# One ones-product per norm: squares of two RMS norms summed off TensorE in a fused two-block kernel

## The reference, cut to what matters

```
x = x + m @ w_o                                          # first block; the kernel calls this X1
gate = sigmoid(rmsnorm(x, ple_norm_g) @ w_ple_gate)      # the norm "r_ple", over 2048 features
x = x + gate * (p @ w_ple_proj)
...
o = (o_f + o_b)                                          # second block: retention, 4 heads of 256 values
o = o * rsqrt(mean(o * o, axis=-1) + 1e-6)               # the norm "rn", one per head, over its 256 values
```

## Time and profile before

| | before |
|---|---|
| median of 3 runs | 2671.77 us (2671.35 to 2673.11) |
| profiled execution | 2669.51 us, of which the span of the trace is 2668.2 us |
| granted TensorE clock, mean | 0.998 of full speed |
| PE busy | 2631.1 us, 99% |
| DVE / ACT / POOL busy | 1276.1 / 888.8 / 91.9 us (48 / 33 / 3%) |

### The profile page before, as it was taken

The page is one execution under the profiler, slowest core; times in us unless marked ns, Lnnn a source line. Parts: engine busy times, 40 slices in busy tenths (PEclk is TensorE's granted clock), DMA queues, the critical chain, the costliest instruction groups (busy, mean ns, idle before and its releaser), DMA issues.

```text
span 2668.2 us, 28964 instructions
## 1 busy us (share of the span) xinstructions
PE 2631.1 (99%) x11830; PEld 2135.4 (80%) x11830; DVE 1276.1 (48%) x1806; ACT 888.8 (33%) x1232; POOL 91.9 (3%) x75
## 2 busy tenths in 40 slices
PE   8999999999999999999999999999999999999998
PEld 6888888888888888888888887778866777777888
DVE  7546634447434555655542263563343334443425
ACT  5633324333323222222232352332232333433323
POOL 4000000000000000000000011100000000000000
PEclk9999999999999999999999999999999999999999
DMA  5322233222233666666443223234312322222424
GB/s 180 103 80 71 79 87 99 84 79 71 87 95 123 209 209 209 201 204 211 142 158 110 88 87 107 83 100 162 95 54 65 95 71 79 72 72 86 160 100 150
DMA packets 159364, 308.07 MB, mean 115 GB/s; under 512 B 10944, under 2 KB 15296, under 8 KB 158208
## 3 DMA queue, kind: packets, MB, share of 16 engines
q1 hardware_dynamic: 158432, 304.65, 35.8%
q0 software_dynamic: 224, 1.15, 0.1%
q10 hardware_dynamic: 576, 0.43, 0.1%
HBM read 297.80 MB, written 8.39 MB: 115 GB/s over the span
## 4 chain that ended last, share of the span: by engine, by line
PE 93%; DVE 3%; issue 2%; ACT 1%; DMA 0%; POOL 0%; SPq 0%; ACTq 0%; DVEq 0%; POOLq 0%
PE bank L329 84%; PE bank L669 2%; PE bank L1205 1%; PE bank L1101 1%; PE bank L1179 1%; PE bank L385 1%; PE bank L688 1%; DVE WL L361 1%; DVE XL L454 1%; PE bank L1194 1%; PE bank L1090 1%; DMA X<-in_xT 0%; PE bank L956 0%; ACT WH L347 0%; DVE Y L1916 0%
## 5 line engine op out<-in xcount | busy, mean ns | idle before, releaser
L329 PE MATMUL bank<-XH,WH 128*128 128x512 f32 (+1 forms) x2880 | 1150.5, 399 | 19.0 <-DVE XL L454 10.6
L329 PE MATMUL bank<-XH,WL 128*128 128x512 f32 (+1 forms) x2880 | 1111.2, 386 | 3.8 <-DVE WL L361 3.8
L329 PE MATMUL bank<-XL,WH 128*128 128x512 f32 (+1 forms) x2880 | 1108.9, 385 | 0.0
L361 DVE TENSOR_TENSOR WL<-RAW,WH 128x1024 fp32r<-128x1024 f32 x444 | 547.7, 1236 | 960.7 <-ACT WH L347 959.9
L347 ACT CAST WH<-RAW 128x1024 fp32r<-128x1024 f32 x444 | 464.2, 1047 | 1202.8 <-PE bank L329 1197.1
L329 PEld LDWEIGHTS bank<-XH,WH 128*128 128x128 f32 x2880 | 542.5, 188 | 139.9 <-issue 31.8
L329 PEld LDWEIGHTS bank<-XL,WH 128*128 128x128 f32 x2880 | 542.8, 188 | 118.4 <-issue 15.8
L329 PEld LDWEIGHTS bank<-XH,WL 128*128 128x128 f32 x2880 | 542.0, 188 | 116.8 <-DVE WL L361 5.5
L329 PE MATMUL bank<-WH,XH 128*128 128x512 f32 x384 | 154.2, 401 | 0.0
L329 PE MATMUL bank<-WL,XH 128*128 128x512 f32 x384 | 149.6, 390 | 0.0
L329 PE MATMUL bank<-WH,XL 128*128 128x512 f32 x384 | 149.4, 389 | 0.0
(11 more groups left out here) (241 smaller groups left out, 1679.8 us busy)
## 6 DMA issues: line engine op xcount, KB each, us to landing
RAW<-in_w_in SPq DMA_DIRECT2D x304, 512.0 KB, 3.6
AST<-in_w_ada SPq DMA_DIRECT2D x192, 256.0 KB, 3.7
RAW<-in_w_out SPq DMA_DIRECT2D x40, 512.0 KB, 3.5
RAW<-in_w_o SPq DMA_DIRECT2D x32, 512.0 KB, 3.6
RAW<-in_w_gate SPq DMA_DIRECT2D x32, 512.0 KB, 3.6
RAW<-in_w_a SPq DMA_DIRECT2D x16, 512.0 KB, 4.1
RAW<-in_w_b SPq DMA_DIRECT2D x16, 512.0 KB, 4.1
XT<-in_xT SPq DMA_DIRECT2D x4, 1024.0 KB, 6.6
```

Source lines behind the costliest of these rows:

```text
L329: ins = nc.tensor.matmul(bank[b][:, cols], l, r[:, cols], start=first, stop=final)
L361: nc.vector.tensor_tensor(WL[:, m % NSPL], RAW[:, m % NRAW], WH[:, m % NSPL].bitcast(F32), ALU.subtract).then_inc(lo.sem, lo.step(m))
```

## The change

For r_ple, POOL also adds the squares of tiles 12 to 15 to `AC[:, 0]` (15 additions in place of 11), and PE does one ones-product, which waits for the last addition. For rn, DVE adds `TN[:, 1]` to `TN[:, 0]` once both squares are there, and PE does one ones-product, which waits for that. The addition has a piece of its own on DVE, two pieces behind the last decay product; the sum and what follows it lie one piece later, so that a head has ten pieces on each of the three engines.

```
@@ retention_pe
             yield
+        yield
         b, was = special_bank(("rn", r), dve, (("rn", r), "m"))
         T.wait_ge(was[0], (yield was))
-        for u in range(2):
-            T.wait_ge(act, (yield act, ("rsq", r, u)))
-            ones_sum(b, TN[:, u], (("rn", r), "sum") if u else None, start=u == 0, stop=u == 1)
+        T.wait_ge(dve, (yield dve, ("rsqs", r)))
+        ones_sum(b, TN[:, 0], (("rn", r), "sum"))
         yield
@@ retention_dve
         yield
+        yield
+        for u in range(2):
+            V.wait_ge(act, (yield act, ("rsq", r, u)))
+        nc.vector.tensor_tensor(TN[:, 0], TN[:, 0], TN[:, 1], ALU.add).then_inc(dve.sem, dve.step(("rsqs", r)))
         yield
         yield
         yield from rsqrt_dve(("rn", r), 1.0 / 256, TN[:, 2], TN[:, 3], TN[:, 0])
@@ pe
-                T.wait_ge(pool, (yield pool, ("acc1", 11)))
-                ones_sum(b, AC[:, 0], None, stop=False)
-                for i in range(4):
-                    T.wait_ge(act, (yield act, ("sq1", 12 + i)))
-                    ones_sum(b, GT[:, i], ("r_ple", "sum") if i == 3 else None, start=False, stop=i == 3)
+                T.wait_ge(pool, (yield pool, ("acc1", 15)))
+                ones_sum(b, AC[:, 0], ("r_ple", "sum"))
@@ pool_program
-        for j in range(1, 12):
+        for j in range(1, 16):
             G.wait_ge(act, (yield act, ("sq1", j)))
             if j > 1:
                 G.wait_ge(pool, (yield pool, ("acc1", j - 1)))
```

## The result

| | before | after |
|---|---|---|
| median, 12 runs each | 2671.94 us (2670.38 to 2673.11) | 2664.85 us (2662.75 to 2666.72) |
| ratio, 95% interval | | 0.9974 [0.9967, 0.9982] |
| profiled execution, span | 2669.51 us, 2668.2 | 2666.04 us, 2664.7 |
| PE busy, PE records of each kind | 2631.1 us, 11830 | 2628.0 us, 11814 |

The kernel became 7.1 us faster (0.26%), where 6.8 us were forecast. But the two profiled executions are only 3.5 us apart in their spans, half of it. That is the question of this study.

The account below looks back on a forecast made before the run. PE was taken as the bound, with no idle time where the change works. Profiled execution: 2669.51 - 6.87 (3.43 r_ple, 3.44 heads) + 0.1 = 2662.7 us; median: 2671.77 - 6.77 = 2665.0 us, -0.25%; range 2663.3 to 2667.4 us.

Parts of the forecast that it names:

- The price of a ones-product: On PE's chain at r_ple and the heads: two records of 0.429 us each, 0.858 us a product, 6.87 us removed together.
- POOL in time: At r_ple's sum: POOL's last addition reaches PE at 1524.76, 0.27 us ahead of the sum's weight load at 1525.03.
- The twin: POOL's four additions for tiles 8 to 11, 6.45 us long, taken whole as the length of those for tiles 12 to 15.
- The 0.1 us of wait in the sum: At r_ple's sum: 0.1 us added to the forecast for PE's queue not running ahead of the semaphore.
- rival (a): At r_ple's sum: POOL is late, PE waits up to 1.84 us, 2666.7 us, -0.19%; chance 0.08.
- DVE's additions and wait: In the heads: four additions of 0.69 us fit DVE's idle time, slack some 3.2 us; its wait holds up nothing.
- (b): In the shifted heads: PE waits for WL or a bank, 4 x 1.0 us lost, 2669.0 us, -0.1%; chance 0.07.
- (c): In the heads: DVE's new wait for the squares starves PE of low parts, slower than before, 2677.2 us; chance 0.02.
- (d): On the chain: idle bits of ACT or DVE close up too, at most 3.1 us of WL waits, 2661.9 us; chance 0.03.
- The longer heads: Four heads take 40 of 48 steps, formerly 36; plain steps behind head 3 shrink from 14 to 10; cost zero.
- What the profile would show: Ones-products: no GT, TN x8; PE 16 matmul records fewer, some 6.9 us less busy; sums 0.86 us; WL ahead of L398.
- What I said would prove me wrong: PE idle ahead of r_ple's sum, new WL or WH waits between 1930 and 2100 us, or gate groups starting no earlier.

## Why the prediction was right, step by step

- **The price of a ones-product, 0.858 us.** Right to the hundredth: 3.43 us at r_ple's sum (4.29 to 0.86), 0.86 at each head. Taking it from the chain and not from the record of 0.592 us was what made it so; two records of 0.592 would have given 1.18 us a product and 9.5 us in all. That the weight loads set this pace, as the prediction has it, is not shown: they stand idle for 0.24 us ahead of each, and they and the matmuls simply come 0.43 us apart.
- **POOL in time.** Right. The twin, tiles 8 to 11, gave 6.45 us; the new four took 6.44, and ended 0.37 us ahead of the weight load (forecast: 0.27 with 0.10 for the signal; from POOL's end to PE's first matmul it is 0.14 us in the experiment with the sum first). The 0.1 us of wait in the sum did not come. The experiment with the sum ahead of `proj` 0 shows that `proj` 0, 5.5 us long, was what lay between a gain of 7 us and none, so rival (a) was rightly priced as the main danger, even if its bound of 1.84 us left out a fall of the clock behind a wait.
- **DVE's additions and wait.** Right. The addition ended at 1947.35, the weight load of the sum came at 1950.4, 3.1 us later (forecast some 3.2). The WL subtraction went ahead of the root at 1949.21 (forecast 1949.3). No PE wait in the heads, so (b) and (c) fall; the WL waits elsewhere are 3.1 us as before, so (d) falls too.
- **The longer heads.** Right: 14 plain steps behind head 3 became 10, and attention starts where it did.
- **The time.** 2665.0 forecast, 2664.85 measured. That it fits to 0.15 us is luck: the interval of the measured gain runs from 4.8 to 8.8 us. The mechanism rests on the chains. (The stated range was also narrower than its own words: the scatter of +1.3 us on the late end, 2666.7, reaches 2668.0, not 2667.4.) One step was not sound: I took the distance of 2.26 us between profiled execution and median as a constant offset. It was mostly the absence of falls of the clock in one lucky execution: with 9 falls in 10 profiles and 4 in 13, an execution has on average 0.90 + 0.31 = 1.2 of them, about 2.0 us by this estimate. The forecast took only the difference to the median, so it did no harm as long as the falls come to both kernels alike. The profiles show both falls in either kernel; thirteen of them are too few to say that they are equally frequent. Had I been asked for the next profile's span, I would have said 2668.2 - 6.8 = 2661.4 and been wrong by 3.3 us.
- **What the profile would show.** One item failed: PE was to be some 6.9 us less busy, and in the first pair it was 3.1. The step left out is the clock: busy time grows by what a fall costs. **What I said would prove me wrong** included nothing about equal work taking longer ahead of the changed place. That was the only odd thing in the profile after, and by the profiles alone, without one more of the old kernel, it would have looked as if the change had lost half its gain.

## What to carry to other kernels

Where TensorE sets the end, a reduction over partitions need be paid on it only once: let an idle engine add the tiles first, as long as its last addition ends ahead of TensorE's arrival, and look for that in a twin of the same additions elsewhere in the trace. Price what is removed by the step in the chain, not by the length of a record. When two single profiles differ by an amount near the effect, find a stretch of equal work that takes unequal time before believing either, and profile the old kernel again.

## What the runs showed of the hardware

- **After a short wait the clock falls in some executions and not in others, and a fall costs about as much as the wait.** Behind a PE wait of 1.8 us the granted clock fell to 0.50 for about 3 us in nine of ten profiles, behind one of 1.2 us in four of thirteen, behind one of 1.1 to 1.2 us near 1690 us in none of the three kernels with spread weights; a fall costs 1.6 us of dense work. The executions with the higher mean clock are on average the faster ones: of the 28 of before on the first chip, the 26 at 0.997 average 2672.3 us and the 2 at 0.998 2671.0. The Trainium skill (TensorE: Matmul & The Clock Gate, "What's actually happening") has the clock depend on how busy the array has been recently; the traces agree, in that each of these falls stands right behind a wait. What decides between fall and no fall behind the same wait, no run here shows.
- **POOL's additions slow DVE's small instructions fourfold.** The kernel after at the end of `gate` 2: two of DVE's `WG` instructions of one line and shape.

```profile
1682.03 1.34 DVE L1870 TENSOR_SCALAR WG<-ONES,V 128x128 f32<-128x128 f32 x1
...
1689.53 0.34 DVE L1870 TENSOR_SCALAR WG<-ONES,V 128x128 f32<-128x128 f32 x1
```

POOL there:

```profile
1678.86 10.66 POOL L1963 TENSOR_TENSOR AC<-AC,SQ 128x512 f32<-128x512 f32 x8 [34.87 <-ACT SQ L1588]
```

POOL's eight additions end at 1689.52, and the instruction at 1689.53 is the first quick one: 0.34 us against 1.34, the latter about the length of one addition (1.29). The Trainium skill (SBUF — State Buffer, "Who interferes with whom") says that `tensor_scalar` can take the ports which DVE shares with GpSimd, and that the one that issues second then stands still; the trace agrees. That is how nine small instructions hold up the low part for which PE waits 1.8 us, with the fall of the clock behind it. Spreading them shortens the wait by only 0.65 us, since the same additions then slow the subtraction itself (1.85 us for 1.22). For r_ple the additions cost DVE nothing that shows: its one subtraction beside them takes 1.23 us (1.22 before), and it is POOL's fourth addition that is long. At the end of `gate` 2 they do cost; no run takes them away there, so how much is not shown.
